# Second layer's first norm: sums by token in two columns, factors spread by TensorE, a modulation piece split around the spread

## What is computed

```
def rmsnorm(x, gain=None):
    y = xf * lax.rsqrt(jnp.mean(xf * xf, axis=-1, keepdims=True) + NORM_EPS)

def trunk_layer(x, cond, lw, lam_init, ropes, ctx):
    mod = (jax.nn.silu(cond) @ lw['w_ada'] + lw['b_ada'])[:, None, :]
    shift1, scale1, gate1, shift2, scale2, gate2 = jnp.split(mod, 6, axis=-1)
    h = rmsnorm(x, lw['norm_mix']) * (1 + scale1) + shift1
    mix, new_ctx = token_mixers(h, lw, lam_init, ropes, ctx)
    x = x + gate1 * (mix @ lw['w_out'])
    h = rmsnorm(x, lw['norm_ffn']) * (1 + scale2) + shift2
    x = x + gate2 * moe_ffn(h, lw)
```

## Time and profile before

| | |
|---|---|
| median of 3 runs | 1336.48 us (1335.72 to 1339.12) |
| profiled execution, its own time | 1338.24 us |
| its span, first to last instruction | 1336.3 us |
| granted TensorE clock, mean | 0.969 of full |
| busy share of the span | PE 92%, PEld 62%, DVE 21%, ACT 18% |
| DMA | 496.58 MB, mean 372 GB/s; about 422 GB/s where it is the bound |

### The profile page before, as it was taken

One profiled execution on the slowest core, in us unless ns is written; L12 is line 12 of the kernel. 1 busy time (PEld: TensorE's weight loads), 2 busy tenths in 40 slices (PEclk: granted clock), 3 DMA queues, 4 the chain that ended last, 5 costly groups with the idle time before them and its releaser, 6 DMA issues.

```text
span 1336.3 us, 22734 instructions
## 1 busy us (share of the span) xinstructions
PE 1225.3 (92%) x9596; PEld 835.2 (62%) x9596; DVE 280.3 (21%) x720; ACT 239.4 (18%) x533; POOL 2.8 (0%) x13
## 2 busy tenths in 40 slices
PE   7999999999998889888999999999999889888986
PEld 4566686667765565556565668766767466556554
DVE  1252362111111010101034425401101010101012
ACT  2363131110010001010134521311010001010102
POOL 0000000000000000000000000000000000000000
PEclk9999999999999999889999999999999899889989
DMA  9888849999999999999956663999999999999992
GB/s 385 335 318 339 352 188 422 399 422 421 421 421 422 422 422 422 420 421 422 395 218 247 251 233 149 418 420 421 421 420 421 421 422 422 422 422 421 423 420 105
DMA packets 80657, 496.58 MB, mean 372 GB/s; under 512 B 10576, under 2 KB 12880, under 8 KB 24784
## 3 DMA queue, kind: packets, MB, share of 16 engines
q1 hardware_dynamic: 76528, 493.63, 90.1%
q10 hardware_dynamic: 4064, 2.00, 0.5%
HBM read 493.60 MB, written 2.00 MB: 371 GB/s over the span
## 4 chain that ended last, share of the span: by engine, by line
PE 68%; DMA 24%; DVE 4%; SPq 2%; issue 1%; ACT 1%; DVEq 0%; ACTq 0%
DMA dn<-in_exp_w_down 18%; PE PS L2205 15%; PE PS L2241 13%; PE PS L2135 8%; PE PS L2142 7%; PE PS L1709 7%; PE PS L2041 4%; DMA gu<-in_exp_w_gate 4%; PE PS L1651 2%; PE PS L1619 2%; DMA gu<-in_w_in 1%; PE PS L2090 1%; PE PS L1832 1%; PE PS L1843 1%; PE PS L2181 1%
## 5 line engine op out<-in xcount | busy, mean ns | idle before, releaser
L2205 PE MATMUL PS<-gu,arena 128*32 128x256 f32 (+1 forms) x3072 | 313.4, 380 | 0.0
L2241 PE MATMUL PS<-arena 128*64 128x512 f32 (+1 forms) x336 | 180.0, 686 | 63.7 <-DMA dn<-in_exp_w_down 62.1
L2205 PEld LDWEIGHTS PS<-gu,arena 128*32 128x32 f32 (+1 forms) x3072 | 182.6, 117 | 79.0 <-issue 18.0
L2241 PE MATMUL PS<-dn,arena 128*32 128x512 f32 (+1 forms) x688 | 187.7, 640 | 0.0
L2135 PE MATMUL PS<-arena 128*128 128x128 f32 x1408 | 176.3, 278 | 0.5 <-ACT arena L1042 0.5
L2135 PEld LDWEIGHTS PS<-arena 128*128 128x128 f32 x1408 | 164.1, 192 | 17.9 <-issue 16.7
L2142 PE MATMUL PS<-arena 128*128 128x256 f32 x704 | 160.2, 380 | 1.4 <-ACT arena L1025 1.4
L2205 PE MATMUL PS<-arena 128*64 128x256 f32 (+1 forms) x672 | 152.0, 379 | 0.0
L2142 PEld LDWEIGHTS PS<-arena 128*128 128x128 f32 x704 | 130.2, 190 | 20.5 <-ACT arena L1025 3.2
L1530 DVE TENSOR_TENSOR arena<-arena,PS 128x256 f32<-128x256 f32 x44 | 18.5, 421 | 563.1 <-ACT arena L1038 563.1
L1025 ACT ACTIVATE arena<-PS 128x512 f32<-128x512 f32 x88 | 52.6, 597 | 462.6 <-PE PS L2241 462.6
(11 more groups left out here) (264 smaller groups left out, 1023.9 us busy)
## 6 DMA issues: line engine op xcount, KB each, us to landing
gu<-in_exp_w_gate SPq DMA_DIRECT2D x106, 1024.0 KB, 15.7
gu<-in_exp_w_up SPq DMA_DIRECT2D x86, 1024.0 KB, 17.6
dn<-in_exp_w_down SPq DMA_DIRECT2D x86, 1024.0 KB, 18.6
arena<-in_exp_w_up SPq DMA_DIRECT2D x42, 1024.0 KB, 14.6
arena<-in_exp_w_down SPq DMA_DIRECT2D x42, 1024.0 KB, 16.2
gu<-in_w_ada SPq DMA_DIRECT2D x20, 2048.0 KB, 8.9
xh<-in_exp_w_gate SPq DMA_DIRECT2D x22, 1024.0 KB, 11.4
gu<-in_w_in SPq DMA_DIRECT2D x8, 2048.0 KB, 13.1
```

What stands on the lines that cost most here:

```text
L2205: ins = mmul(PS[w * h:w * h + w, 5, FF * half:FF * half + FF], xg[:, k, w * h:w * h + w], weights[half][:, k], start=(k == 0), stop=(k == ...
L2241: ins = mmul(PS[w * h:w * h + w, 7 - n, :], hidT[:, j * P + w * h:j * P + w * h + w], weights[:, j, 512 * n:512 * n + 512], start=(j == 0) ...
```

## The change

Norm k = 2 takes the form of the expert norms. Its sums are 16 matmuls of 2 columns instead of 8 of 256, root and reciprocal are of 128x2, and TensorE spreads the factors (`spread`, now a function of its own, called by both kinds of norm). The modulation piece's 8 matmuls are cut in two halves of four, with the spread between them. Two semaphore counts follow from that.

```diff
@@ ScalarE, norm(k)
-                sums = (small[:, 0:G], PS[:, 5, 0:2 * G:2]) if k % 2 else (small[:, 0:T], PS[:, 5, 0:T])
+                sums = (small[:, 0:G], PS[:, 5, 0:2 * G:2]) if k > 0 else (small[:, 0:T], PS[:, 5, 0:T])
@@ ScalarE, end of the kernel (VectorE has the same line)
-            act.wait_ge(S["rstd_ready"], DEPTH + 1)
+            act.wait_ge(S["rstd_ready"], 2 * DEPTH)
@@ VectorE, norm(k)
-                if k % 2:
+                if k > 0:
                     v.reciprocal(small[:, G:2 * G], small[:, 0:G]).then_inc(S["rstd_ready"], 1)
-
-                    link(v.tensor_copy(shift_sum, PS[:, 2, 0:G * E]))
-                    v.wait_ge(S["rstd_spread"], l + 1)
+                    if k % 2:
+
+                        link(v.tensor_copy(shift_sum, PS[:, 2, 0:G * E]))
+                    v.wait_ge(S["rstd_spread"], k)
                     factors = PS[:, 5, T:2 * T]
@@ TensorE, ada(n, flush=False, between=None)
                                    start=(quarter == 0 and c == 0), stop=(quarter == 3 and c == 1))
+                    if c == 0 and between is not None:
+                        between()
                 ins.then_inc(S["weights_used"], 1)
@@ TensorE
+            def spread(k):
+
+                pe.wait_ge(S["rstd_ready"], k)
+                for g in range(G):
+                    ins = mmul(PS[:, 5, T + g * P:T + g * P + P], small[:, G + g:G + g + 1].to_broadcast([P, P]), ident,
+                               start=True, stop=True)
+                ins.then_inc(S["rstd_spread"], 1)
+
             def norm(k):
-                        ins = mmul(PS[:, 5, 0:T], C("ones"), hT[:, c], start=(c == 0), stop=(c == NC_ - 1))
+                        if k == 0:
+                            ins = mmul(PS[:, 5, 0:T], C("ones"), hT[:, c], start=(c == 0), stop=(c == NC_ - 1))
+                        else:
+                            for g in range(G):
+                                ins = mmul(PS[:, 5, 2 * g:2 * g + 2], hT[:, c, g * P:g * P + P], C("ones", 2),
+                                           start=(c == 0 and g == 0), stop=(c == NC_ - 1), skip_group_check=True)
                     ins.then_inc(S["ss_ready"], 1)
-                    if k in ADA_NORM:
-                        ada(ADA_NORM[k])
+                    if k > 0:
+                        ada(ADA_NORM[k], between=lambda: spread(k))
                     return
```

More of the change, by code:

```diff
@@ L1606, in _ @@
             v.reciprocal(small[:, 6:8], small[:, 6:8]).then_inc(S["rstd_ready"], 1)
-            v.wait_ge(S["rstd_ready"], DEPTH + 1)
+            v.wait_ge(S["rstd_ready"], 2 * DEPTH)
             stt(y_tok[:, 1].rearrange("p (t c) -> p t c", c=NC_), by_token(1), small[:, 7:8], gain, ALU.mult,
@@ L1637, in ada_select, with ada @@
                 ins.then_inc(S["ada_sel"], 1)
-            def ada(n, flush=False):
+            def ada(n, flush=False, between=None):
                 w = piece(items_ada[n])
@@ L1694, in norm @@
                 routed(range(4, 6))
[L1696 to L1700, removed]
+                spread(k)
                 routed(range(6, NC_)).then_inc(S["router_done"], 1)
```

## The result

The changed kernel took 1340.1 us, median of 18 runs (1338.08 to 1342.05), and the kernel before 1337.28 on the same chip, also of 18 runs (1335.72 to 1342.37). The ratio is 1.0017, 95% interval [1.0011, 1.0024]: some 2.3 us slower (1337.28 x 0.0017; the two medians differ by 2.82), where the prediction had 0.9 us faster and a range up to 1338.4, above which 1340.1 lies. (The kernel before came out higher too, by 0.8, than the 1336.48 that the prediction started from.) The loss is smaller than the 0.3% that the prediction took for its line, but it is clear of noise and has the other sign.

The account below looks back on a forecast made before the run. The chain was taken as 68% TensorE and 24% DMA, the norm as a place where TensorE waits; first product at 685.43 instead of 686.30 gains 0.87, so 1336.48 - 0.87 = 1335.6 us, range 1334.2 to 1338.4.

Parts of the forecast that it names:

- half of it 0.93, so the spread can start at 683.74 + 0.93 = 684.67: On TensorE at the norm: the half modulation piece takes 0.93 us and releases the spread 0.28 after the reciprocal's end.
- The prediction's own sign of being wrong: At the norm: the forecast is wrong if the spread starts later than 685.0; it was expected at 684.67.
- Cost nothing: Verdict on products read from PSUM and on the second half piece, with 0.4 us cover; the sums likewise, hidden by the table load.
- the sixth: Anywhere: an effect that no row shows, worth more than 0.3% either way; chance 0.05.
- Sums hidden by the table load: At the norm: the new sums end at 683.71, before the table is ready at 683.92, so they cost and gain nothing.
- rival 3: At the norm: sums outlast the table load, first product at 687.0 or so, 0.7 later than now, 1337.2 us; chance 0.06.
- Root 0.26 and reciprocal 0.17: At the norm: root 0.26 us instead of 0.47, reciprocal 0.17 instead of 1.75, starting 0.03 after the root; gain 1.87.
- Products from PSUM at 0.41: VectorE's products with the factors at the norm: 411 ns from PSUM against 416 ns from SBUF, cost nothing.
- rival 4: VectorE's eight products at the norm: each 0.065 us slower from PSUM, gain only 0.35, 1336.1 us; chance 0.05.
- rival 5: Between 687 and 833 us: the saved time is lost in a wait that does not move, 1336.5 us; chance 0.07.
- The bounds of 0.6 and 1.0: Lower and upper limit, in us, of the 0.87 gain forecast at the norm's first product.
- Rival 2: After the last landing: TensorE's clock rises no earlier, so half the gain is lost, 0.44 left, 1336.0 us; chance 0.13.

Follow-up runs that it names:

- e2: Changed kernel plus 54 matmuls in the second layer's never-entered overflow branch, code behind it 256 instructions later than in the kernel before: ratio 1.005, 1344.61 us.
- e5: Changed kernel with 10 matmuls left out of the second layer's never-entered overflow branch, so code behind it stands where it was: ratio 1.0003, 1339.11 us.
- e1: Kernel before plus 10 matmuls that never run, in the second layer's overflow branch, code behind it 40 instructions later: ratio 1.0004, 1338.83 us.
- e10: Changed kernel with 128-column sums and 20 extra matmuls per pair round in both layers' expert loops, 200 instructions more: ratio 1.0028, 1341.13 us.
- e4: Changed kernel with 128-column sums and 54 matmuls in the second layer's never-entered overflow branch, 256 instructions more: ratio 1.0038, 1343.3 us.
- e9: Changed kernel with 128-column sums and 20 extra matmuls per pair round in the second layer's expert loop, 120 instructions more: ratio 1.0031, 1342.02 us.

## Why the prediction was wrong

**Its sum failed in one silent term.** All of TensorE's durations were taken at a granted clock of 1.00, from the earlier trace rows, for a stretch in which the new sums stand right ahead. The step that failed is "half of it 0.93, so the spread can start at 683.74 + 0.93 = 684.67". The half lasted 1.86 and the spread 1.22. The prediction's own sign of being wrong, a spread that starts later than 685.0 (2.36 behind the table load), came: it started at 2.90. In the profiles with two-column sums (after, e2, e5) the clock fell at the norm in 3 of 3, in the eight with 128 columns in none, and in the five profiles of the old form not until the first projections, and there only in e1. The earlier trace rows could not stand for this place: the expert norm's sum is 4 records of two columns (L1692, x4; VectorE has added up the eight chunks before, and TensorE sums one) between records of 64 columns, and its spread took 0.66 at a clock of 1.00. Here 32 records of two columns come in one run, 4.07 us long. So the prediction took the price of the form from a run an eighth as long. Whether the length of the run makes the difference was not tested.

**"Cost nothing" failed for the instructions themselves.** The prediction priced each added matmul where it runs. The 40 instructions cost 1.6 us where they don't: 620 us later, behind a jump. This is the greater part of the loss, and it alone would have turned a gain of 0.87 into a loss of 0.7. None of the six cases covers it: the sixth, "something that none of these rows shows", had 0.05, but for more than 0.3%, and this is 0.12%.

**What held.** Sums hidden by the table load: the root starts 0.01 behind it, so rival 3 falls. (Its price was also summed wrong: with sums that end at 685.6 the half piece still stands ahead of the spread, which gives 685.6 + 0.93 + 0.76 = 687.3 for the first product and not 687.0.) Root 0.26 and reciprocal 0.17; the reciprocal starts 0.10 behind the root and not 0.03, which the half piece hides. Products from PSUM at 0.41, so rival 4 falls, and with it the figure of the Trainium skill that was weighed there ("VectorE: DVE Perf Modes", the TRN2 errata): no run here shows the extra 0.065 us. The path from norm to L623: what the first product gains or loses arrives there to within 0.03 in every run but e1, in which 0.9 is lost between the two (there the clock was 0.50 from 687 to 690 us, behind the 1.8 us idle wait that the old form has), and from there to the last landing it took 449.3 before and after, so rival 5 falls. With the clock up the gain was 0.79 where the sum had 0.87: the half piece takes 1.00, not 0.93, and the rest is 0.01. The bounds of 0.6 and 1.0 held it.

**Rival 2** has its place right: the 16 records at the landing took from 5.01 (e5) to 6.63 us, without order between kernels, and 3.65 where TensorE was kept at work. It looks like the scatter that the prediction named. With one profile of each kernel a small share in the loss isn't excluded.

## What to carry to other kernels

Price a new run of matmuls at the clock that it leaves behind, not only by its pitch: here eight weight loads took 0.99 us with two columns and 0.97 with 128, and only the wider form kept the clock. Look, too, how long the run was in the row that a price is taken from. When a small change to one place loses time, compare the profile stretch by stretch to the very end: "issue" of a microsecond amid a loop's matmuls meant here that something in the place of the code was at fault, and then the question is how many instructions the change put ahead of a jump. Test it by adding code that never runs; and of two versions whose times differ by 0.1%, don't judge by time alone before that is excluded.

## What the runs showed of the hardware

- TensorE's granted clock fell to 0.50 after 32 two-column matmul records with 128x128 weight loads, with at most 0.11 us idle in any window of 1 us from the sums to the fall (after, e2, e5), between 0.1 us ahead of the sums' end and 0.8 us behind it, and cost 0.5 to 1.3 us against the wide form. The same 32 records with 128 columns were followed by 1.00 in eight profiles of eight, and so were the 4 two-column records of the expert norm in the earlier trace rows.
- A jump over code that isn't entered can be followed by a stop of TensorE, from none to 4.24 us, whose place is fixed in the code: 20, 40 and 60 more instructions ahead of the target put it after 30, 20 and 10 matmul records. It lasted 0.51, 1.09 to 1.57, 1.87, 3.83, 1.83 and 4.1 to 4.2 us at +20, +40, +60, +120, +200 and +256, and in all of these but +200, and in e10's first layer (4.10 us at +80), it ended 3.3 to 4.2 us after the round's start. For +200 I have no explanation.
- From about the end of the stops of 3.8 to 4.2 us the granted clock was 0.50 for some 3 us, and the next 32 records took 5.06 to 5.36 us in place of 3.60 (e2, e4, e9, and the first layer of e10).
- The page of the changed kernel has the queue that fetches code, 0.84 MB in 51 packets, 16 KB each (0.84 / 51); the row is the same in the kernel before, and in the four kernels with +120 and more it is 52 packets and 0.85 MB:

```profile
q8 instruction: 51, 0.84, 0.2%
```

The Trainium skill, "Runtime: NRT & Kernel Launch", section "Instruction fetch mechanics", says that code comes in blocks of 16 KiB, 256 instructions, ahead of need and in sequence, and that a taken branch to a target outside what is held must wait for a fetch. The size of the packets and the stop behind the jump agree with it; that the stop is this wait is an inference, since no view shows single fetches. How much code TensorE holds, and why a whole block of padding (+256) made the stop longer and not the same, no run here shows.
